# Page numbers read earlier, page sums and a cache copy moved, and the first pair's rows picked with the one-hot stationary

## The chip, the cores and the metric

The kernel runs on one core of a Trainium2 chip. The metric is the device time in microseconds (us) of one execution. The program is one hand-scheduled instruction stream per engine: TensorE (PE), VectorE (DVE), ScalarE (ACT), GpSimd (POOL) and SyncE (SP). SP issues nearly all DMAs and computes nothing. Engines wait for each other by semaphores only. All tensors are float32.

## The reference, cut to what matters

One inference step of a two-layer decoder over 264 tokens (T = 264): a prompt of 256 and 8 sample tokens. Layer 0 mixes with a state-space block, layer 1 with sparse attention (NSA), which reads a paged cache. Each layer ends in the same tail: a layer norm, a mixture of 16 experts with two experts per token, a second layer norm, and a gated per-layer embedding.

```python
def layer_tail(x, mix, p_i, ...):
    h = layer_norm(DEEPNORM_ALPHA * x + mix, ln1_g, ln1_b)
    h = layer_norm(DEEPNORM_ALPHA * h + moe(h, ...), ln2_g, ln2_b)
    return h + jax.nn.sigmoid(h @ ple_gate) * (p_i @ ple_proj)

# moe: for each expert e of 16, D = 1024, FF = 512
hid = jax.nn.silu(h @ w_gate[e]) * (h @ w_up[e])
out = out + gate[..., e:e + 1] * (hid @ w_down[e])

# layer 1, sample tokens: 8 pages of 128 rows per sequence, blocks of 64 rows
past_cmp = kv_pool[page_table, :, 0:2]
kvc = jnp.einsum('bnlckd,clk->bnckd', blocks, w)      # weighted sum over each block
```

The window cache of layer 1 comes back with its oldest row dropped and the new one added. The 511 old rows per sequence are an output copied straight from the input.

## The kernel before, in words

`tail(L)` (from L947) is run for L = 0, then the NSA stage (from L1544), then `tail(1)`. Each of these is one block: all engines meet at its end before the next begins.

A tail goes like this. The first layer norm and the router run first (L1058 to L1110). PE turns the normed activations into token rows (`turn_x`, L1072, which the trace shows as L1080), ACT copies them to SBUF (`xtok`) and stores them to the DRAM tensor `x_rows` (L1283). DVE works out, for every expert, which of 64 slots each token takes, and writes that as a one-hot matrix `sel1` (`onehot`, L1421), columns by expert and slot.

The experts are then done in 8 pairs. A pair's 128 slots need their tokens' activations as `xg` (features on the partitions, slots along the free axis). For the first pair PE gets them at once from `xtok` and `sel1` (L1115 to L1120, traced as L1119): for each of 8 feature chunks, three matmuls over the three token tiles, `xtok` as the stationary operand and 128 one-hot columns moving, which gives features by slots. ACT copies each half (4 chunks, one PSUM bank `gb[a]`) into `xg` (`pack`, L1292). For later pairs, PE computes the slots' token numbers (`slot_token`, L1108), DVE turns them into integers (`slot_gates`, L1428), POOL gathers the rows from `x_rows` with an indirect DMA (L1347), and PE turns them (`turn_rows`, L1141). The token numbers of pairs 0 and 1 are computed by six small matmuls between the first pick and the first gate product (L1121 to L1126). Those of later pairs are computed inside `up(i)`, one after each of its last steps.

Each pair is `gate(i)` (L1158, 8 steps of k, each two experts side by side in half the array's columns), `up(i)` (L1177), `turn(i)` (L1186) and `down(i)` (L1199); the result is scattered to the tokens by `scatter(i)` (L1209), added up by DVE (L1460). PE's order is in the loop at L1218. The weights come in 2 MB units through a ring of eight places. SP issues unit n + 8 when unit n's place is free, in program order (L1014 to L1028): units 8 and 9 wait for `gu_half`, which `gate(0)` signals after k = 3.

After the pairs come the second layer norm and the per-layer gate: PE makes eight tiles (L1255, m = 0 to 7), DVE takes each tile (L1523, L1524), ACT applies the sigmoid (L1336), DVE finishes the tile of `xT` (`finish`, L1514, L1516). PE may start tile m = 6 once DVE has taken tile 1.

In `tail(0)` three things for the NSA stage are mixed in. SP, after the last `down`, reads 16 page numbers from SBUF into registers (`page_number`, L1042) and loads the 8 pages of sequence 0 (`load_cmp`, L132) and two chunks of the NSA weights (L99), then, after e_done 4, the pages of sequence 1. DVE multiplies the pages of sequence 0 by the block weights (`cmp_multiply`, L136, four of them) between centring and the reciprocal of the second norm (L1502 to L1508), and sums them (`cmp_sum`, L140) one after each of the tiles m = 2 to 5. The semaphore `c_used` counts sequences summed; later page loads in the NSA stage wait for it, the ones of sequences 3 and 4 for `c_used` 1 and 2.

The NSA stage begins with DVE's loop over sequences 1 to 6 (`compress`, from L2010), POOL's multiplications for it (L136) and PE's 21 projection tiles (L1709). In `tail(1)` SP issues the copy of the old window rows, DRAM to DRAM (`win_old`, 8176 KB, L1030) after the last weights; the program's last block waits for it.

Of the kernel before, what the change touches and what calls it, by code (L numbers as in the profile page):

```python
# [20 lines left out]
P = 128  # L21
D = 1024
# [36 lines left out]
def trunk(nc, I, O):  # L59
    root = ExitStack()  # L60
    with root:
        def sem(name):
            return root.enter_context(nc.semaphore(name))
# [84 lines left out]
        router_sems = [sem("r_" + n) for n in ("log", "sig", "turn", "gate", "rank", "slots", "xtr", "xtok", "idx", "tok", "rows", "got", "over", "evac", "row0", "row1")]  # L148
# [798 lines left out]
        def tail(L, out=None):  # L947

            ld_p, e_done, e_sig, e_out, e_proj, e_pre, e_evac = ple_sems
            r_log, r_sig, r_turn, r_gate, r_rank, r_slots, r_xtr, r_xtok, r_idx, r_tok, r_rows, r_got, r_over, r_evac, r_row0, r_row1 = router_sems  # L950
# [4 lines left out]
            with ExitStack() as st:  # L955
# [26 lines left out]
                ohid = over[:, 3 * T:(3 + NF) * T].rearrange("p (f t) -> p f t", f=NF)  # L982
                rs, sgm = sgt[:, 0:2, :], sgt[:, 2:4, :]
# [28 lines left out]
                with nc.Block() as block:  # L1012
                    @block.sync
                    def _(sp):  # L1014
                        load_unit(sp, L, 3 * L, unit(3 * L))
                        sp.wait_ge(gu_half, L + 1)
# [12 lines left out]
                        if L == 1:  # L1029
                            sp.dma_start(O["win_old"], I["cache_win"][:, 1:, :]).then_inc(win_out, 16)  # L1030
# [10 lines left out]
                        if L == 0:  # L1041
                            page = [page_number(sp, n) for n in range(2 * NPG)]  # L1042
# [12 lines left out]
                    def _(pe):  # L1055
# [59 lines left out]
                        for a in range(2):  # L1115
                            for k in range(4):
                                d = 4 * a + k
                                for q, (t0, n) in enumerate(tile3):
                                    last = mm(gb[a][:, k * P:(k + 1) * P], xtok[q][0:n, d * P:(d + 1) * P], sel1[0:n, q, 0:P], start=q == 0, stop=q == 2)  # L1119
                            last.then_inc(gathered, 1)  # L1120
                        pe.wait_ge(r_gate, 2 * L + 2)  # L1121
                        pe.wait_ge(r_slots, 6 * L + 4)
                        for i in range(2):
                            for q in range(3):
                                last = slot_token(i, q, ob[0], i * (1 + NE))
                        last.then_inc(r_idx, 1)  # L1126
# [20 lines left out]
                        def gate(i):  # L1147
# [6 lines left out]
                            for k in range(KD):  # L1154
# [5 lines left out]
                                if i == 0 and k == 3:  # L1160
                                    last.then_inc(gu_half, 1)
                            last.then_inc(gu_done, 1)
# [130 lines left out]

# [1025 lines left out]
```

## Time and profile before

| | |
|---|---|
| three runs | 1116.6, 1119.33, 1121.22 us; median 1119.33 |
| profiled execution | 1118.43 us, span 1116.7 us |
| mean granted TensorE clock | 0.966 of full |
| busy share of the span | PE 93%, TensorE weight loads 57%, DVE 44%, ACT 27%, POOL 15% |
| DMA moved | 346.33 MB, mean 310 GB/s |

A busy share is a mean over stages of quite different kinds. PE's 93% says that for most of the span the time is PE's; the slices in which PE is not busy, or has half the clock, or does work of low value, are where other engines matter. The timeline lists instructions of each engine by start and duration, merged where they follow each other, and says in brackets how long the engine had been idle and who ended that.

### The profile page before, as it was taken

How to read it: one execution, taken by the hardware profiler on the slowest of the kernel's cores; microseconds unless marked ns; L12 is line 12 of the kernel's file. 1: busy time of each engine (PE TensorE's matmuls, PEld its weight loads, DVE VectorE, ACT ScalarE, POOL GpSimd, SP SyncE). 2: the span in 40 equal slices, each digit the busy share in tenths (PEclk: the TensorE clock that was granted, in tenths of full speed). 3: DMA queues.
4: the chain of work that ended last, by engine and by line, in shares of the span. 5: the costliest groups of instructions: out<-in, count | busy, mean ns of one | idle time of the engine just before them, and what ended most of it. 6: DMA issues, size and time to landing. Idle time of an engine off the chain costs nothing. (4 is left out here: it accounts for less than half of the span.)

```text
span 1116.7 us, 15016 instructions
## 1 busy us (share of the span) xinstructions
PE 1036.7 (93%) x5267; PEld 639.4 (57%) x5267; DVE 494.3 (44%) x1473; ACT 306.3 (27%) x785; POOL 167.8 (15%) x163
## 2 busy tenths in 40 slices
PE   7999998699999999999896999788999999999987
PEld 5788776488763444444475885344775443444456
DVE  1759798582531111111276996672162111111136
ACT  3111688910321111111132104462051111111124
POOL 0000002420000000000142833553000000000023
PEclk9899999899989999999998998999999999999999
DMA  9645598569429999999774975976984999999974
GB/s 317 220 160 188 154 282 276 197 226 395 189 77 396 427 429 425 428 427 427 297 301 164 394 247 166 326 244 219 428 345 151 403 429 425 428 427 426 429 313 204
DMA packets 89537, 346.33 MB, mean 310 GB/s; under 512 B 14770, under 2 KB 52658, under 8 KB 72402
## 3 DMA queue, kind: packets, MB, share of 16 engines
q1 hardware_dynamic: 82202, 321.94, 74.3%
q10 hardware_dynamic: 5240, 16.03, 3.9%
q0 software_dynamic: 2016, 7.34, 1.7%
q8 instruction: 45, 0.74, 0.3%
q14 instruction: 34, 0.28, 0.1%
HBM read 330.61 MB, written 23.04 MB: 317 GB/s over the span
## 5 line engine op out<-in xcount | busy, mean ns | idle before, releaser
L1460 DVE TENSOR_TENSOR acc<-acc,mo 128x264 f32<-128x264 f32 x64 | 27.5, 429 | 239.0 <-PE mo L1209 238.3
L518 PE MATMUL ss<-xT,expert_ring 128*128 128x264 f32 x384 | 92.9, 404 | 7.1 <-DMA expert_ring<-in_ssd_w_in 7.1
L1199 PE MATMUL mo<-expert_ring,gates_and_hidden 128*64 128x512 f32 x384 | 85.0, 595 | 8.2 <-ACT gates_and_hidden L1306 8.2
L1177 PE MATMUL mh<-expert_ring,x_packed 128*64 128x512 f32 x384 | 91.6, 603 | 0.0
L1158 PE MATMUL mh<-expert_ring,x_packed 128*64 128x512 f32 x384 | 89.1, 618 | 0.4 <-DMA expert_ring<-in_moe_w_gate 0.2
L518 PEld LDWEIGHTS ss<-xT,expert_ring 128*128 128x128 f32 x384 | 75.8, 200 | 21.4 <-issue 7.8
L1709 PE MATMUL na<-xT,expert_ring 128*128 128x264 f32 (+1 forms) x336 | 77.3, 394 | 11.2 <-PEq L1012 11.2
L1347 POOL DMA_INDIRECT x_rows_packed<-x_rows,slot_token_int x14 | 13.5, 961 | 476.6 <-DVE slot_token_int L1428 256.7
L1709 PEld LDWEIGHTS na<-xT,expert_ring 128*128 128x128 f32 (+1 forms) x336 | 64.1, 191 | 24.3 <-issue 11.9
L1469 DVE TENSOR_TENSOR gates_and_hidden<-mh,silu_gate 128x512 f32<-128x512 f32 x16 | 11.1, 691 | 132.8 <-PE mh L1177 132.8
L530 PE MATMUL ss<-xT,expert_ring 128*128 128x264 f32 x256 | 62.9, 400 | 6.3 <-ACT expert_ring_b L409 6.3
L1158 PEld LDWEIGHTS mh<-expert_ring,x_packed 128*64 128x64 f32 x384 | 29.1, 142 | 57.3 <-issue 57.2
L1199 PEld LDWEIGHTS mo<-expert_ring,gates_and_hidden 128*64 128x64 f32 x384 | 26.5, 137 | 59.1 <-issue 48.0
L530 PEld LDWEIGHTS ss<-xT,expert_ring 128*128 128x128 f32 x256 | 48.4, 194 | 19.5 <-ACT expert_ring_b L409 9.8
L1306 ACT ACTIVATE gates_and_hidden<-mo 128x512 f32<-128x512 f32 x16 | 9.6, 597 | 179.9 <-PE mo L1186 179.9
L634 PE MATMUL ss<-conv_out,expert_ring 128*128 128x264 f32 x224 | 51.4, 386 | 0.7 <-issue 0.7
L634 PEld LDWEIGHTS ss<-conv_out,expert_ring 128*128 128x128 f32 x224 | 42.5, 190 | 8.1 <-issue 0.9
L1315 ACT ACTIVATE y_slots<-mo 128x512 f32<-128x512 f32 x32 | 17.4, 594 | 101.3 <-PE mo L1199 101.3
L1209 PE MATMUL mo<-gates_and_hidden,y_slots 128*128 128x264 f32 x128 | 41.5, 406 | 3.9 <-issue 3.9
L1177 PEld LDWEIGHTS mh<-expert_ring,x_packed 128*64 128x64 f32 x384 | 24.0, 136 | 36.3 <-issue 35.5
L1255 PE MATMUL mo<-slot_onehot,expert_ring 128*128 128x266 f32 x192 | 44.4, 387 | 0.0
L136 POOL TENSOR_TENSOR expert_ring<-expert_ring,pos_softmax 128x1024 f32<-128x1024 f32 x14 | 39.0, 2811 | 23.8 <-DMA expert_ring<-in_cmp_pages 23.8
(419 smaller groups left out, 1844.2 us busy)
## 6 DMA issues: line engine op xcount, KB each, us to landing
expert_ring<-in_moe_w_down SPq DMA_DIRECT2D x24, 2048.0 KB, 18.0
expert_ring<-in_moe_w_gate SPq DMA_DIRECT2D x24, 2048.0 KB, 19.0
expert_ring<-in_moe_w_up SPq DMA_DIRECT2D x20, 2048.0 KB, 21.0
expert_ring<-in_ssd_w_in SPq DMA_DIRECT2D x9, 2048.0 KB, 7.9
expert_ring<-in_cmp_pages SPq DMA_DIRECT2D x40, 256.0 KB, 5.5
expert_ring_b<-in_moe_w_gate SPq DMA_DIRECT2D x4, 2048.0 KB, 17.4
expert_ring_c<-in_moe_w_gate SPq DMA_DIRECT2D x4, 2048.0 KB, 21.9
expert_ring<-in_moe_w_up SPq DMA_DIRECT2D x8, 1024.0 KB, 7.3
```

The source lines that it names most:

```text
L136: return eng.tensor_tensor(x, x, wb[:, a:a + 1, :].unsqueeze(1).to_broadcast([P, NPG, 2, BLK]), ALU.mult)
L518: last = mm(pt[m % 4][:, 0:T], wc[:, k, ((m - 1) % 4) * P:((m - 1) % 4 + 1) * P], xT[:, k, :], start=k == 0, stop=k == KD - 1)
L530: last = mm(z_bank[:, 0:T], wc[:, k, (j % 4) * P:(j % 4 + 1) * P], xT[:, k, :], start=k == 0, stop=k == KD - 1)
L634: last = mm(o_bank[m][:, 0:T], w_row(k)[:, m * P:(m + 1) * P], cv[:, k, :], start=k == 0, stop=k == JX - 1)
L1158: last = mm(hb[0][s * CAP:(s + 1) * CAP, :], xg[:, k, s * CAP:(s + 1) * CAP], unit(6 * i + s)[:, k * FF:(k + 1) * FF], start=k == 0, stop= ...
L1177: last = mm(hb[1][s * CAP:(s + 1) * CAP, :], xg[:, k, s * CAP:(s + 1) * CAP], unit(6 * i + 2 + s)[:, k * FF:(k + 1) * FF], start=k == 0, s ...
L1199: last = mm(ob[2 + a][s * CAP:(s + 1) * CAP, :], ht[:, k, s * CAP:(s + 1) * CAP], unit(6 * i + 4 + s)[:, o:o + 512], start=k == 0, stop=k ...
L1209: mm(sc_bank[d % 4][:, 0:T], ys[:, d * P:(d + 1) * P], sgt[:, i, :], start=True, stop=True).then_inc(sc_done, 1)
L1255: last = mm(gate_bank[m % 6][:, 0:T + 2], wc[:, k, (m % 4) * P:(m % 4 + 1) * P], scaled[:, k, :], start=k == 0, stop=k == KD - 1)
L1315: A_(ys[:, a * 512:(a + 1) * 512], ob[2 + a][:], ACT.Copy).then_inc(ys_ok, 1)
L1460: V.tensor_tensor(acc[:, d, :], acc[:, d, :], sc_bank[d % 4][:, 0:T], ALU.add).then_inc(acc_ok, 1)
L1709: last = mm(pb[m % 8][0:M, 0:T], wc[:, k, (m % 4) * P:(m % 4) * P + M], xT[:, k, :], start=k == 0, stop=k == KD - 1)
```

## The change

Five edits.

1. The first pair's rows are picked the other way round: the one-hot (128 columns) is stationary and 512 features of the token rows move, three matmuls for each half. The result is slots by features. ACT copies each half to SBUF (`x0`, a free part of `mixed`), PE turns it with four transposes into the same PSUM bank, and the old `pack` follows.
2. The six `slot_token` matmuls of pairs 0 and 1 move from before `gate(0)` into it, one after each of k = 0 to 5.
3. The copy of the old window rows is issued by SP at the start of `tail(0)`, right behind the first weight unit, not near the end of `tail(1)`.
4. SP reads the 16 page numbers right after the last weight loads of `tail(0)`, before it waits for the last `down`.
5. The four page sums of sequence 0 move from the tiles m = 2 to 5 of `tail(0)` to the start of the NSA stage, ahead of DVE's `memset`s.

```diff
                         load_unit(sp, L, 3 * L, unit(3 * L))
+                        if L == 0:
+                            sp.dma_start(O["win_old"], I["cache_win"][:, 1:, :]).then_inc(win_out, 16)
                         sp.wait_ge(gu_half, L + 1)
...
                             load_unit(sp, L, n, unit(n))
-                        if L == 1:
-                            sp.dma_start(O["win_old"], I["cache_win"][:, 1:, :]).then_inc(win_out, 16)
+                        if L == 0:
+                            page = [page_number(sp, n) for n in range(2 * NPG)]
...
                         if L == 0:
-                            page = [page_number(sp, n) for n in range(2 * NPG)]
                             load_cmp(sp, 0, page)
...
                         for a in range(2):
+                            for q, (t0, n) in enumerate(tile3):
+                                last = mm(gb[a][:], sel1[0:n, q, 0:P], xtok[q][0:n, a * 512:(a + 1) * 512], start=q == 0, stop=q == 2)
+                            last.then_inc(r_picked, 1)
+                        for a in range(2):
+                            pe.wait_ge(r_first, 2 * L + a + 1)
                             for k in range(4):
-                                d = 4 * a + k
-                                for q, (t0, n) in enumerate(tile3):
-                                    last = mm(gb[a][:, k * P:(k + 1) * P], xtok[q][0:n, d * P:(d + 1) * P], sel1[0:n, q, 0:P], start=q == 0, stop=q == 2)
+                                last = tr(gb[a][:, k * P:(k + 1) * P], x0[:, (4 * a + k) * P:(4 * a + k + 1) * P], ident[:])
                             last.then_inc(gathered, 1)
-                        pe.wait_ge(r_gate, 2 * L + 2)
-                        pe.wait_ge(r_slots, 6 * L + 4)
-                        for i in range(2):
-                            for q in range(3):
-                                last = slot_token(i, q, ob[0], i * (1 + NE))
-                        last.then_inc(r_idx, 1)
...
                                 if i == 0 and k == 3:
                                     last.then_inc(gu_half, 1)
+                                if i == 0 and k < 6:
+                                    if k == 0:
+                                        pe.wait_ge(r_gate, 2 * L + 2)
+                                        pe.wait_ge(r_slots, 6 * L + 4)
+                                    slots = slot_token(k // 3, k % 3, ob[0], k // 3 * (1 + NE))
+                                    if k == 5:
+                                        slots.then_inc(r_idx, 1)
...
+                        for a in range(2):
+                            act.wait_ge(r_picked, 2 * L + a + 1)
+                            A_(x0[:, a * 512:(a + 1) * 512], gb[a][:], ACT.Copy).then_inc(r_first, 1)
                         pack(0)
...
-                            if L == 0 and 2 <= m < 6:
-                                i1 = cmp_sum(V, 0, m - 2)
-                                if m == 5:
-                                    i1.then_inc(c_used, 1)
...
+                    for a in range(4):
+                        i1 = cmp_sum(V, 0, a)
+                    i1.then_inc(c_used, 1)
                     V.memset(kcx[:], 0.0)
```

## Rows read from the trace of the kernel before

**Rows 1.** Timeline of layer 0's first pick (start us, us, engine, line, operation, tiles).
```profile
315.08 0.61 PE L1119 MATMUL mg<-slot_onehot,x_rows_packed 128*128 128x128 f32 x4
...
319.30 0.60 ACT L1292 ACTIVATE x_packed<-mg 128x512 f32<-128x512 f32 x1 [3.63 <-PE mg L1119]
...
323.41 2.34 PE L1108 MATMUL mo<-token_and_gates,slot_onehot 128*128 128x17 f32 x12
...
335.35 4.46 PE L1177 MATMUL mh<-expert_ring,x_packed 128*64 128x512 f32 x20
```

**Rows 2.** Timeline of layer 1, the same stretch.
```profile
839.30 0.61 PE L1119 MATMUL mg<-slot_onehot,x_rows_packed 128*128 128x128 f32 x4
...
857.99 4.46 PE L1177 MATMUL mh<-expert_ring,x_packed 128*64 128x512 f32 x20
```

**Rows 3.** Chain that ended last (start us, us, what): one whole `up`, full clock.
```profile
1028.46 7.02 PE mh L1177 x32
```

**Rows 4.** Timeline: two slot_token matmuls inside up(0), and the router's transposes.
```profile
306.93 1.04 PE L1080 MATMUL mg<-ident,xT 128*128 128x128 f32 x8
...
339.74 0.40 PE L1108 MATMUL mo<-token_and_gates,slot_onehot 128*128 128x17 f32 x2
...
341.07 0.40 PE L1108 MATMUL mo<-token_and_gates,slot_onehot 128*128 128x17 f32 x2
```

**Rows 5.** Windows: length, busy us of PE, PEld, DVE, ACT, POOL, clock, DMA share, GB/s.
```profile
305.00:310.00 5.00, 5.00 (x37) 4.38 (x36) 4.52 (x22) 4.60 (x12) 0.00 (x0) 1.00 0.03 12
...
324.00:325.00 1.00, 1.00 (x7) 0.97 (x6) 0.00 (x0) 0.98 (x2) 0.00 (x0) 0.71 0.00 0
...
850.00:855.00 5.00, 5.00 (x20) 1.40 (x16) 4.42 (x5) 0.00 (x0) 0.94 (x1) 0.66 0.36 105
```

**Rows 6.** Timeline of layer 0's end, SP and ACT.
```profile
522.16 0.80 SPq L112 DMA_DIRECT2D expert_ring<-in_ple_gate  x2
...
549.44 1.08 ACT L1315 ACTIVATE y_slots<-mo 128x512 f32<-128x512 f32 x2 [7.19 <-PE mo L1199]
...
559.82 3.97 SPq L132 DMA_DIRECT2D expert_ring<-in_cmp_pages  x8
```

**Rows 7.** Timeline of layer 0's second norm and gate tiles.
```profile
567.36 0.48 ACT L1330 ACTIVATE gates_and_hidden<-mh,eps 128x264 f32<-128x264 f32 x1 [1.29 <-PE mh L1262]
...
569.05 4.63 DVE L136 TENSOR_TENSOR expert_ring<-expert_ring,pos_softmax 128x1024 f32<-128x1024 f32 x4 [4.74 <-DMA expert_ring<-in_cmp_pages]
...
573.72 1.80 DVE L1508 RECIPROCAL slot_onehot<-gates_and_hidden 128x264 f32<-128x264 f32 x1
...
577.94 7.35 PE L1255 MATMUL mo<-slot_onehot,expert_ring 128*128 128x266 f32 x32
...
582.29 1.21 DVE L140 TENSOR_REDUCE cmp_dec<-expert_ring 128x16 f32<-128x1024 f32 x1
...
595.68 0.43 DVE L1516 TENSOR_TENSOR xT<-gates_and_hidden,acc 128x264 f32<-128x264 f32 x1
...
596.44 3.86 PE L1709 MATMUL na<-xT,expert_ring 128*128 128x264 f32 x8 [11.15 <-PEq L1012]
```

**Rows 8.** Chain that ended last: layer 1's last two gate tiles, last piece.
```profile
1103.68 7.20 PE mo L1255 x32
...
1113.06 0.43 DVE xT L1516
```

**Rows 9.** Timeline of the NSA stage: DVE's multiplications for sequence 2.
```profile
613.79 4.52 DVE L136 TENSOR_TENSOR expert_ring<-expert_ring,pos_softmax 128x1024 f32<-128x1024 f32 x2 [7.33 <-DMA expert_ring<-in_cmp_pages]
```

**Rows 10.** Windows, as in Rows 5.
```profile
310.00:320.00 10.00, 10.00 (x62) 8.29 (x61) 2.59 (x15) 3.72 (x9) 0.00 (x0) 1.00 0.27 102
...
1080.00:1090.00 10.00, 10.00 (x46) 8.45 (x45) 6.23 (x11) 4.13 (x11) 6.12 (x9) 1.00 0.49 210
```

**Rows 11.** Timeline, SP: layer 0's first weight unit.
```profile
290.77 0.34 SPq L112 DMA_DIRECT2D expert_ring<-in_moe_w_gate  x1
```

**Rows 12.** The gathers, L1347: POOL's issue to landing.
```profile
DMA to landing us min/median/max: 4.6/11.6/12.5
```

More of the change, by code:

```diff
@@ L147, in trunk @@
         ln_total, ln_squares, ln_inv = [sem("ln_" + n) for n in ("total", "squares", "inv")]
-        router_sems = [sem("r_" + n) for n in ("log", "sig", "turn", "gate", "rank", "slots", "xtr", "xtok", "idx", "tok", "rows", "got", "over", "evac", "row0", "row1")]
+        router_sems = [sem("r_" + n) for n in ("log", "sig", "turn", "gate", "rank", "slots", "xtr", "xtok", "idx", "tok", "rows", "got", "over", "evac", "picked", "first", "row0", "row1")]
         moe_sems = [sem("m_" + n) for n in ("gather", "packed", "gate_half", "gate_up", "silu", "hid", "turned", "ht", "down", "ys", "scatter", "acc")]
@@ L949, in tail @@
             ld_p, e_done, e_sig, e_out, e_proj, e_pre, e_evac = ple_sems
-            r_log, r_sig, r_turn, r_gate, r_rank, r_slots, r_xtr, r_xtok, r_idx, r_tok, r_rows, r_got, r_over, r_evac, r_row0, r_row1 = router_sems
+            r_log, r_sig, r_turn, r_gate, r_rank, r_slots, r_xtr, r_xtok, r_idx, r_tok, r_rows, r_got, r_over, r_evac, r_picked, r_first, r_row0, r_row1 = router_sems
             gathered, packed, gu_half, gu_done, silu_ok, hid_ok, turned, ht_ok, down_done, ys_ok, sc_done, acc_ok = moe_sems
@@ L982, in tail @@
                 ohid = over[:, 3 * T:(3 + NF) * T].rearrange("p (f t) -> p f t", f=NF)
+                x0 = mixed[:, NP2 * T:NP2 * T + D]
                 rs, sgm = sgt[:, 0:2, :], sgt[:, 2:4, :]
```

## The prediction

> **What bounds the kernel now.** I read the chain of waits first, then the waits by engine, then the timelines of the stretches that the diff touches. The chain is PE from pair to pair: one `up` is 7.02 us of matmuls [rows 3], the other parts of a pair follow without a gap, and no weight load makes PE wait for more than a fraction of a microsecond. So in the pairs only what PE itself does counts. Three stretches are different. From the first pick to the first `up`, PE takes 335.35 - 315.08 = 20.3 us in layer 0 and 857.99 - 839.30 = 18.7 us in layer 1 [rows 1, 2], part of it at a lower clock: in the windows at 324 and at 850 the mean falls to 0.71 and 0.66, that is to the 1.2 GHz level for part of each, right when PE does the small `slot_token` matmuls and begins the gate [rows 5]. And at layer 0's end PE is done with its last gate tile at 577.94 + 7.35 = 585.3, yet starts the next stage at 596.44; DVE works until 595.68 + 0.43 = 596.1 [rows 7]. There DVE is the bound, for 11 us. Layer 1's same tail has no such tail: PE ends at 1103.68 + 7.20 = 1110.9, DVE at 1113.5, 2.6 us later [rows 8].
>
> **Edits 1 and 2, the first pick and the slot numbers.** Before, 24 matmuls of 128 columns, 48 instructions, 323.41 - 315.08 = 8.3 us, each at the price of loading 128 columns of weights; then 12 instructions of `slot_token`, 2.34 us [rows 1]; then the gate, which is 335.35 - 325.75 = 9.6 us where 16 matmuls at full clock take 7.0 [rows 3]. After: 6 matmuls, 12 instructions of 512 columns over the full width. In an `up` 32 instructions run two by two in 7.02 us, so one costs 0.43 us alone [rows 3], and 12 cost 5.2 us. ACT's copy of the first half (0.60 us [rows 1]) lies beside the second half's matmuls. The second copy does not: a handover of 0.1, 0.6, the last four transposes (half of 1.04 us for eight [rows 4]) beside the first `pack`, which itself is 0.6. The gate starts about 1.5 us after the last pick, at 6.7 us from the start.
> The six slot matmuls inside the gate: in `up(0)` two steps with one each lie 341.07 - 339.74 = 1.33 us apart [rows 4], a bare step is 7.02 / 8 = 0.88, so one costs 0.45 to 0.5 and six 2.8 us. That is more than the 1.8 to 2.3 us of doing them in one run, but nothing waits at half clock meanwhile. Gate 7.0 + 2.8 = 9.8. Sum 6.7 + 9.8 = 16.5 us. Against 20.3 and 18.7 this saves 3.8 us in layer 0 and 2.2 us in layer 1, if the clock stays at the 2.4 GHz level. If PE falls to 1.2 GHz within this stretch, as it does now, the loss comes back that the gate shows now: 9.6 - 7.0 = 2.6 us in layer 0, and some 1.6 in layer 1 (18.7 less 8.3 for the picks, 1.8 for the slot matmuls and 7.0). Then 1.2 us are saved in layer 0 and 0.6 in layer 1. I take the full clock, since the densest kind of matmul replaces the sparsest and the run of `slot_token` is gone. Bounds for both layers together: 0 (the clock low for longer than now) and 6.5 us.
> What speaks against it is the stretch with the new transposes. In the window from 305 to 310, PE did little but the router's transposes, three groups of eight, and was granted the full clock throughout [rows 4, 5]. The Trainium skill (TensorE: Matmul & The Clock Gate, Part 4: PE-mode transpose) says that transposes do not count as PE-busy the way matmuls do. By that rule, the eight transposes and the waits around them would be an idle 1.5 us, and the gate could start cold; by the row they are harmless. The row decides for me, and the rule is the first rival below.
> The slot numbers come later: `r_idx` moves from the end of the run (325.75) to gate step 5, 6.7 + 6 x 1.33 = 14.7 us after the start, 329.8, so 4 us later in layer 0 and about 4.5 in layer 1. DVE's `slot_gates`, the wide `onehot` and POOL's first gather queue behind it. The gather lands 4.6 us after issue with an idle DMA, 11.6 with weights in flight [rows 12]; it is needed after `up(0)`, at 331.6 + 8.4 + 0.5 = 340.5. Issued at 330.3 it lands between 334.9 and 341.9. I take 0.5 us of waiting over both layers, with bounds 0 and 3.
> `gu_half` comes at 6.7 + 4 x 1.33 = 12 us from the start, 5 us earlier than now; the weights start that much earlier too. No gain by itself, as PE does not wait for them.
>
> **Edit 4, page numbers.** SP is free from 523 (its last weight issue is at 522.16) and PE's last `down` ends at 549.4, but the first page load is issued at 559.82 [rows 6]: 10.4 us, nearly all of it 16 register reads. DVE waits 4.74 us for the pages, multiplies for 4.63 us and only then takes the reciprocal at 573.72, though the square root it needs was done at 567.36 + 0.48 [rows 7]. After: the reads fill SP's free time, the load is issued near 550.5 and lands, 9.2 us later as now, near 560. DVE multiplies from 564.3, where its centring ends (573.72 - 4.63 - 4.74 = 564.35), meets POOL's additions for part of it (two multiplications took 4.52 us beside POOL [rows 9], against 4.63 for four), and is done near 569.5. The reciprocal comes 4.2 us earlier.
>
> **Edit 5, the page sums.** Four reductions of 1.21 us, 1.13 from start to start of the next instruction, go from DVE between tiles 2 and 5: 4.5 us [rows 7]. With the 4.2 us above, DVE would be 8.7 us ahead, and PE is the bound: its tiles do not move, since tile 6 needs only tile 1 taken. PE ends at 585.3, DVE 2.6 us later as in layer 1 [rows 8], and the next stage's first matmul comes 0.3 us after that: 588.2 for 596.44. Saved: 8.2 us. Neither edit alone would reach that.
> What they cost in the NSA stage: DVE starts with 4.6 us of sums. It now waits 7.33 us for sequence 2's pages [rows 9], which SP loads from the stage's start and which do not depend on the sums, so the 4.6 us are hidden. `c_used` 1 is waited for by ACT, which first reads eight page numbers (some 4.5 us by the price above), and `c_used` 2 by SP behind its own reads and loads; each is late by 1 us at most. Taken as 0; if the cover were gone, 4.6 us.
> A smaller gain: PE now starts the stage after 11.15 us of idleness at half clock, 8 matmul instructions in 3.86 us [rows 7], and loses some 2 us. With 2.9 us of idleness instead it starts at full clock or comes back sooner. I take 1 us, with bounds 0 and 2.2.
>
> **Edit 3, the old rows.** In layer 1 they move at 210 GB/s with nothing beside them [rows 10]; 8.37 MB take 38 to 40 us and end around 1112, beside the first stores of y. In layer 0 they would be issued at 291, right behind the first unit [rows 11], and run until about 334. The DMA engines are nearly idle there (102 GB/s from 310 to 320 [rows 10], which is the store of `x_rows`). The cover ends at `gu_half`, 327: units 8 and 9 queue behind the last 7 us of the copy. They are needed by `up(1)` near 360, so nothing waits. At the end of layer 1, the last y store meets less traffic: 0.3 us, with bounds 0 and 1.
>
> **Sum.** 3.8 + 2.2 - 0.5 + 8.2 + 1.0 + 0.3 = 15.0 us. The profiled execution took 1118.43 us (span 1116.7 and 1.7 around it): 1103.4. It lies 0.9 us below the median of the runs, so from the median 1104.3. I say 1104. The bounds of the terms together: gain 5 to 19.
>
> **Rivals.**
> A. The clock falls in the first gate anyway, in both layers, or at the NSA stage's start. For it: it falls there now, and a wait and transposes are put just before the gate; the rule above. Against it: the row with three groups of transposes at full clock. Price 2.6 us in layer 0, 1.6 in layer 1 and part of the 1 us at the NSA stage: 1108.5.
> B. The tail's gain is given back in the NSA stage: the next stage's start is DVE's and the pages' (the loads for sequences 3 and 4 wait for `c_used`), and PE's earlier start only makes it wait before the first scores. For it: DVE there works from 613.79 on nearly without rest until PE's last projection tile. Against: its start is set by a load that the sums do not touch. Price 4.6 us: 1109.
> C. The copy of the old rows hurts, and the kernel gets slower. The place is layer 0 from 310 to 360: `x_rows` stores, the first gather and units 8 to 11 share the DMA engines with it. The Trainium skill (DMA: Bandwidth & Descriptors, Queues, rings and completion order) says that a semaphore increment lands only after every earlier write of that DMA engine, across its queues; no row here shows it. Worked out from rows: if the `x_rows` stores counted as done only with the copy, at 334, the gather would land at 346 and PE wait 5 us, 1109. It becomes a loss only if the copy holds back units 8 and 9 until more than 15 us after 360, that is if it ran until 370, at half of the 210 GB/s. Then 1119.3 + 1 or more: 1121.
> D. Edits 4 and 5 do not do what they say, because the page load waits for something else (the weight queue at 550). The windows show the queue empty from 550; the load then lands late, and only edit 5's 4.5 us are saved: 1108.
>
> **How the numbers follow.** Forecast 0.56; A 0.18; B 0.09; C mild 0.05, C as a loss 0.03; D 0.04; other misses of the kind that I can't place 0.05, half of them no change. The forecast's own range is 1100 to 1107, A, B and D reach to 1112. With the spread of the runs before (4.6 us) I give 1098.5 to 1111. Below 0.5% (5.6 us, what a measurement of this kernel can tell) no change is seen: faster means under 1113.7. Faster 0.92, same 0.04, slower 0.04.
>
> **What would show it.** In the new trace: 12 pick instructions in 5.2 us, and first pick to first `up` 16.5 us in both layers, with the granted clock at 1.00; no wait of PE for the gathered rows of pair 1; first page load near 1 us after the last `down`; reciprocal right behind the multiplications; PE's first NSA matmul 3 us after its last gate tile, for 11; DVE still waiting for sequence 2's pages. Wrong would be: a clock at 1.2 GHz in the gate (A), PE idle before the first scores (B), PE waiting on weights or rows around 340 to 365 in layer 0 (C), a late page load (D).

## The result and the profile after

The changed kernel took 1126.63 us (median of 8 runs, 1123.45 to 1132.10), the kernel before 1118.33 us beside it (8 runs, 1116.60 to 1121.22): a ratio of 1.0070, with the interval 1.0049 to 1.0091. It is 0.7% slower. The prediction was 1104 us with a range up to 1111, and 0.92 for faster; it was wrong, in sign too. The profiled execution took 1124.01 us, its span 1122.2 us, for 1116.7 before.

The page of the changed kernel: busy time of the engines, then the granted clock and the bandwidth in 40 slices (28 us each).

```profile
span 1122.2 us, 14908 instructions
...
PE 1032.4 (92%) x5211; PEld 629.2 (56%) x5211; DVE 499.2 (44%) x1473; ACT 308.1 (27%) x789; POOL 169.8 (15%) x163
...
PEclk9899999899996999999999998999999999999999
```

The reader should see one 6 in the clock's row, at the thirteenth slice (337 to 365 us). The waits of PE by line say why (us in total, times, longest):

```profile
PE mg L1140 <- DMA x_rows_packed<-x_rows,slot_token_int: 14.0, 1, 14.0
PE mo L1205 <- ACT gates_and_hidden L1315: 11.0, 16, 0.7
```

The second row is old and made of 16 short waits. The first is new, one wait of 14.0 us, for pair 1's gathered rows in layer 0. PE's timeline of layer 0 (start us, us, engine, line, operation, tiles, and in brackets the idle time before it) answers to [rows 1, 4] up to the gate's slot matmuls, and then shows that wait:

```profile
315.30 1.88 PE L1119 MATMUL mg<-x_rows_packed,slot_onehot 128*128 128x512 f32 x4
317.11 1.12 PE L1119 MATMUL mg<-y_slots,slot_onehot 8*128 8x512 f32 x2
318.16 1.98 PE L1119 MATMUL mg<-x_rows_packed,slot_onehot 128*128 128x512 f32 x4
320.08 1.12 PE L1119 MATMUL mg<-y_slots,slot_onehot 8*128 8x512 f32 x2
321.13 1.42 PE L1124 MATMUL mg<-ident,gates_and_hidden 128*128 128x128 f32 x8
322.56 1.08 PE L1157 MATMUL mh<-expert_ring,x_packed 128*64 128x512 f32 x4
323.57 0.40 PE L1110 MATMUL mo<-token_and_gates,slot_onehot 128*128 128x17 f32 x2
...
332.33 4.46 PE L1183 MATMUL mh<-expert_ring,x_packed 128*64 128x512 f32 x20
...
340.72 0.49 PE L1131 MATMUL mo<-ident,gover 128*16 128x128 f32 x3
355.21 1.97 PE L1140 MATMUL mg<-ident,x_rows_packed 128*128 128x128 f32 x8 [14.00 <-DMA x_rows_packed<-x_rows,slot_token_int]
356.97 1.06 PE L1192 MATMUL mo<-ident,gates_and_hidden 128*128 128x128 f32 x4
358.72 8.80 PE L1205 MATMUL mo<-expert_ring,gates_and_hidden 128*64 128x512 f32 x32 [0.69 <-ACT gates_and_hidden L1315]
```

Windows of the same place, with the columns of [rows 5]. The copy of the old window rows is under way from 291 to 340:

```profile
315.00:320.00 5.00, 5.00 (x13) 1.78 (x11) 0.00 (x0) 0.99 (x3) 0.00 (x0) 1.00 0.52 222
320.00:325.00 5.00, 4.88 (x22) 1.95 (x21) 0.00 (x0) 3.06 (x4) 0.00 (x0) 1.00 0.46 196
...
345.00:350.00 5.00, 0.00 (x0) 0.00 (x0) 0.00 (x0) 0.00 (x0) 1.54 (x2) 0.51 1.00 417
350.00:355.00 5.00, 0.00 (x0) 0.00 (x0) 0.00 (x0) 0.00 (x0) 0.00 (x0) 0.50 1.00 406
355.00:360.00 5.00, 4.11 (x16) 2.95 (x18) 0.00 (x0) 1.57 (x3) 0.00 (x0) 0.50 0.53 225
```

The DMA share is about 0.5 while only the copy runs: half of the 16 engines. Then PE does nothing, falls to the 1.2 GHz level (0.50) and works on at it: the `down` from 358.72 takes 8.80 us, where one at full clock takes 7.09.

Where the whole difference lies is seen when both timelines are cut at the same operations of PE. The columns no_move and wide_copy are two of the experiments below. All are us of one profiled execution; each column adds up to its span.

| stretch of PE | before | after | no_move | wide_copy |
|---|---|---|---|---|
| start to first pick, layer 0 | 315.08 | 315.30 | 315.95 | 315.61 |
| first pick to `up(0)` | 20.27 | 17.03 | 17.03 | 17.03 |
| to the turning of pair 1's rows | 8.81 | **22.88** | 8.81 | 8.82 |
| to the first gate tile of the tail | 210.10 | 213.00 | 211.41 | 211.30 |
| gate tiles to NSA's first matmul | 42.18 | 35.70 | 37.38 | 37.39 |
| NSA stage | 218.59 | 221.82 | 219.22 | 223.69 |
| layer 1 to its first pick | 24.27 | 24.26 | 24.27 | 24.27 |
| first pick to `up(0)` | 18.69 | 17.03 | 17.03 | 17.03 |
| to the first gate tile of the tail | 222.16 | 219.13 | 219.55 | 220.13 |
| to the end | 36.51 | 36.09 | 39.03 | 36.11 |

The stretches that edits 1, 2 and 4, 5 touch (first pick to `up(0)`, gate tiles to NSA) have become shorter; one stretch of 9 us has grown by 14.

### The profile page after: what moved, and what is told of

It reads as the page before. It is cut to its first block and busy times, and to the rows that moved or that the text cites. A ratio compares the mean times of both kernels' runs of the same rounds, so it can differ in the third digit from the quotient of the medians.

```text
span 1122.2 us, 14908 instructions
## 1 busy us (share of the span) xinstructions
PE 1032.4 (92%) x5211; PEld 629.2 (56%) x5211; DVE 499.2 (44%) x1473; ACT 308.1 (27%) x789; POOL 169.8 (15%) x163
## 5 line engine op out<-in xcount | busy, mean ns | idle before, releaser
L1157 PEld LDWEIGHTS mh<-expert_ring,x_packed 128*64 128x64 f32 x384 | 26.8, 137 | 47.8 <-issue 47.4
L1183 PEld LDWEIGHTS mh<-expert_ring,x_packed 128*64 128x64 f32 x384 | 24.0, 136 | 36.3 <-issue 35.4
```

Of the source, the lines that this page charges most:

```text
L1157: last = mm(hb[0][s * CAP:(s + 1) * CAP, :], xg[:, k, s * CAP:(s + 1) * CAP], unit(6 * i + s)[:, k * FF:(k + 1) * FF], start=k == 0, stop= ...
L1183: last = mm(hb[1][s * CAP:(s + 1) * CAP, :], xg[:, k, s * CAP:(s + 1) * CAP], unit(6 * i + 2 + s)[:, k * FF:(k + 1) * FF], start=k == 0, s ...
```

## The cause: what holds the gathered rows

My theory was edit 3. The gather reads `x_rows` from DRAM, so POOL may issue it only when the stores of `x_rows` have landed. POOL's timeline of the changed kernel:

```profile
344.49 1.11 POOL L1356 DMA_INDIRECT x_rows_packed<-x_rows,slot_token_int  x1 [108.83 <-DMA x_rows<-y_slots]
```

and that of the kernel before:

```profile
326.24 1.12 POOL L1347 DMA_INDIRECT x_rows_packed<-x_rows,slot_token_int  x1 [90.79 <-DVE slot_token_int L1428]
```

Before, the last thing that POOL waits for is the slot numbers, after it is a store. ACT issues the stores at the same time as ever, and SP has issued the copy 18 us earlier:

```profile
291.37 0.82 SPq L1018 DMA_DIRECT2D out_win_old<-in_cache_win  x1
```

```profile
309.25 0.33 ACTq L1289 DMA_DIRECT2D x_rows<-x_rows_packed  x1
...
312.21 0.29 ACTq L1289 DMA_DIRECT2D x_rows<-y_slots  x1
```

The trace's single packets, summed for each queue over 5 us (q1 is SP's queue, q10 ACT's, the stores; q8 carries instructions), show what happens in between:

```
310: q1: x16 1.05MB mean 2441ns max 2559; q10: x151 0.55MB mean 143ns max 162
315: q1: x16 1.05MB mean 2417ns max 2460; q10: x16 0.07MB mean 159ns max 159
320: q1: x14 0.92MB mean 2422ns max 2488; q10: x16 0.07MB mean 159ns max 159
325: q1: x18 0.83MB mean 1925ns max 2495; q8: x1 0.02MB mean 1778ns max 1778; q10: x14 0.06MB mean 159ns max 159
330: q1: x141 2.01MB mean 564ns max 2998; q10: x12 0.05MB mean 147ns max 166
```

The copy moves packets of 64 KB, 2.42 us each, 8 at a time. On the 8 engines without the copy, the stores are done in 2 us (their increments come at 311.7 to 313.3). On each of the other 8, one store packet of 4 KB (0.16 us) passes for one packet of the copy: 16 against 16 from 315 to 320, 16 against 14 behind that. `x_rows` is 264 rows of 4 KB, some 16 packets for each engine, and in the 20 us from 315 to 335 a loaded engine gets only 7 of them through (58 in the list, over 8). The rest goes when the copy thins out (its last 64 KB packet ends at 339.6), and the last increment comes at 343.7. The Trainium skill (DMA: Bandwidth & Descriptors, Queues, rings and completion order) says that each DMA engine takes turns between its queues packet by packet; these counts agree. The same page (Why a DMA increments its semaphore by 16 and not by 1) says that a DMA is spread over the largest number of engines, at most 16, that divides its slowest dimension, here 8 sequences; the trace agrees with its half share and its 8 loaded engines. I had not read the 210 GB/s of [rows 10] in that way.

Three rivals were still open: the wait comes from the other edits, by chance in one execution (a); the copy is at fault, but through the completion rule of the prediction's rival C, that is, the stores' completion counts only once the copy has ended (b); the copy's bandwidth as such is at fault (c).

### no_move: the changed kernel without edit 3

```diff
-                        if L == 0:
-                            sp.dma_start(O["win_old"], I["cache_win"][:, 1:, :]).then_inc(win_out, 16)
...
+                        if L == 1:
+                            sp.dma_start(O["win_old"], I["cache_win"][:, 1:, :]).then_inc(win_out, 16)
```

> The changed kernel with edit 3 undone (the copy of the old rows back in layer 1). Theory S (sharing: on the 8 DMA engines that carry the copy, each 4 KB packet of the x_rows stores waits for a 64 KB packet of the copy, 2.42 us, so the first gather can't start before 344): with the copy away, the 14.0 us wait of PE for the gathered rows and the 2.9 us of half clock behind it go, about 1107 to 1109. Theory T (the copy is innocent, the later slot numbers of edit 2 make the gather late): the wait stays near 14 us, about 1125. My prediction's sum for the other four edits was 14.7 us below the kernel before, 1104.

Measured: 1113.41 us (1110.08 to 1119.75, 12 runs), ratio to before 0.9966 (0.9947 to 0.9985). In its trace POOL issues the gather at 331.76, and PE does not wait for the rows. Without edit 3, 13 us come back, and (a) falls. The time expected was 1107 to 1109: the wait went, as the theory says, but the other edits gave less than was counted for them (below).

### move_only: the kernel before with edit 3 alone

The same two edits the other way round, on the kernel before.

> The kernel before with edit 3 alone. S: the x_rows stores are complete at about 344 for 314, the gather is issued at 344.5 for 326.2 and lands near 355, PE waits about 11 us before turn_rows(1) and then runs at half clock for a while (5 to 9 us lost): 1134 to 1139. T: the gather is issued at 326 as before and nothing changes: 1118.

Measured: 1132.28 us (1129.97 to 1135.56, 5 runs), ratio 1.0137 (1.0118 to 1.0157). That is 14 us for the edit alone, a little under the 1134 expected. The wait is there without any of the other edits; PE's waits by line:

```profile
PE mg L1141 <- DMA x_rows_packed<-x_rows,slot_token_int: 13.7, 1, 13.7
```

### wide_copy: the changed kernel, the copy on 16 engines, at the same early place

```diff
-                            sp.dma_start(O["win_old"], I["cache_win"][:, 1:, :]).then_inc(win_out, 16)
+                            for b in range(DB):
+                                dst, src = (x.rearrange("r c -> (r c)").rearrange("(a n) -> a n", a=16) for x in (O["win_old"][b], I["cache_win"][b, 1:, :]))
+                                sp.dma_start(dst, src).then_inc(win_out, 16)
```

> The changed kernel, the copy at the same early place but as 8 DMAs of 16 rows of 65408 B, so on all 16 DMA engines. S: at 27 GB/s for each engine the copy takes 20 us and is over near 317; the x_rows stores are complete by 320, before the gather is issued at 331; no wait, 1107 to 1109. If the copy is bound by something that 16 engines share (DRAM writes), it takes 38 us as now, now delays all 16 engines' stores, and the time stays at 1126.

Measured: 1110.94 us (1108.57 to 1113.14, 6 runs), ratio 0.9935 (0.9919 to 0.9950), 2 us above the range expected and still the lowest median of all versions. Windows from 290 on:

```profile
290.00:300.00 10.00, 8.65 (x38) 6.80 (x37) 5.47 (x21) 2.83 (x8) 0.00 (x0) 1.00 0.80 314
300.00:310.00 10.00, 9.86 (x57) 6.25 (x57) 9.24 (x31) 8.55 (x19) 0.00 (x0) 1.00 1.19 408
310.00:320.00 10.00, 10.00 (x47) 6.47 (x44) 3.05 (x18) 4.26 (x9) 0.00 (x0) 1.00 1.02 339
320.00:330.00 10.00, 9.88 (x44) 3.82 (x44) 0.00 (x0) 3.07 (x4) 0.00 (x0) 1.00 0.36 114
```

The copy's packets run from 297.7 to 323.9, 26 us where the changed kernel's take 42 (297.5 to 339.6), the stores are done at 326.1, and POOL issues the gather at 331.43, behind the slot numbers. The same bytes at the same place, moved 1.6 times as fast, make PE wait for nothing, so (c) falls as well: it is not the bandwidth. The stores are held here too. Most of them (170 of 264 rows) go only once the copy is over, 12 us later than before; it does no harm because that is still 5 us before the slot numbers.

### small_eight: the same early copy, still on 8 engines, in pieces of 4088 bytes

```diff
-                            sp.dma_start(O["win_old"], I["cache_win"][:, 1:, :]).then_inc(win_out, 16)
+                            dst, src = (x.rearrange("b r c -> b (r c)").rearrange("b (a n) -> b a n", a=128) for x in (O["win_old"], I["cache_win"][:, 1:, :]))
+                            for h in range(2):
+                                sp.dma_start(dst[:, :, 1022 * h:1022 * h + 1022], src[:, :, 1022 * h:1022 * h + 1022]).then_inc(win_out, 16)
```

> The changed kernel, the copy at the same early place and on the same 8 engines, in descriptors of 4088 B. S: the stores share each engine packet by packet with packets of their own size, and are complete by about 318 though the copy runs until about 335; no wait of PE for rows beyond 2 us, 1107 to 1110. Rival O (a store's completion is held back until the earlier writes of the same engine, across its queues, are done): the stores complete only when the copy ends, 335 or later, PE waits as now, 1122 or more.

Measured: 1150.75 us (1146.51 to 1152.71, 5 runs), ratio 1.0299 (1.0280 to 1.0318). Neither expectation had this time. The stores are no longer too late: they are done at 324.0, and POOL issues the gather at 331.22, behind the slot numbers, while the copy runs on until 372; PE waits 1.1 us for the rows. So a store's completion does not wait for the end of the copy, and (b) falls in the form in which I had used the rule. The changed kernel's own trace says the same: on its loaded engines the first store's increments come at 334.6 to 336.9, the copy's at 338.8 to 340.1. What counts is how long one packet of the neighbour is. But this kernel pays elsewhere. PE's waits by line, then SP's issues:

```profile
PE mh L1185 <- DMA expert_ring<-in_moe_w_up: 19.7, 1, 19.7
...
PE mh L1159 <- DMA expert_ring<-in_moe_w_gate: 7.8, 4, 2.7
```

```profile
327.79 25.99 SPq L112 DMA_DIRECT2D expert_ring<-in_moe_w_up  x4
353.82 5.04 SPq L112 DMA_DIRECT2D expert_ring<-in_moe_w_down  x2
```

Small pieces make the copy slow (130 to 150 GB/s in the windows at 300 and 320, stores included), the weight units queue behind it in SP's queue, and four issues of SP take 26.0 us, in the changed kernel 5.66. That is the prediction's rival C in its form as a loss, "if the copy holds back units 8 and 9". In the changed kernel itself the units were in time.

## Experiments on the other edits

### picks_only: the kernel before with edits 1 and 2

> The kernel before with edits 1 and 2 alone. From the changed kernel's trace these give 3.2 us in layer 0 and 1.7 us in layer 1 from first pick to first up: 1118.3 - 5 = 1113.3. Rival: the gain is lost again in the pairs (later gather, weights asked for earlier while the DMA queue is full): 1118.

```diff
+                            for q, (t0, n) in enumerate(tile3):
+                                last = mm(gb[a][:], sel1[0:n, q, 0:P], xtok[q][0:n, a * 512:(a + 1) * 512], start=q == 0, stop=q == 2)
...
+                                if i == 0 and k < 6:
...
+                                    slots = slot_token(k // 3, k % 3, ob[0], k // 3 * (1 + NE))
```

Measured: 1118.17 us (1116.90 to 1121.31, 12 runs), ratio 0.9998 (0.9987 to 1.0010). Nothing is gained, the rival's number, though the trace shows the two stretches shortened as in the changed kernel (`up(0)` at 332.29 for 335.35, and 17.03 us from pick to `up` in layer 1). Part of the gain goes to the late copy. Its first packets come right behind the last weights, and from its issue to its last packet pass some 67 us in each of these kernels:

| | copy issued | its last packet | last gate tile ends | last store of y issued | end |
|---|---|---|---|---|---|
| before | 1045.6 | 1112.2 | 1110.9 | 1113.5 | 1116.7 |
| picks_only | 1044.0 | 1111.5 | 1107.9 | 1110.6 | 1115.1 |
| no_move | 1038.8 | 1106.0 | 1101.7 | 1104.3 | 1109.7 |

PE's last tile comes 2.9 us earlier in picks_only, the end only 1.5 us, so the copy takes 1.4 us. The rest is lost earlier: the NSA stage takes 2.3 us more than before in this trace, and in layer 0 the pairs behind `up(0)` 1.5 us more. The last thing for which SP waits at the end is the copy; that wait of SP in no_move, then in picks_only:

```profile
SPq L2220 <- DMA out_win_old<-in_cache_win: 1.5, 1, 1.5
```

```profile
SPq L2220 <- DMA out_win_old<-in_cache_win: 0.7, 1, 0.7
```

### wide_only and picks_wide: the same question without the late copy

wide_only is the kernel before with the wide early copy of wide_copy; picks_wide adds edits 1 and 2 to it.

> The kernel before with only the copy moved to layer 0, as 8 DMAs over all 16 DMA engines. Theory S: no wait in layer 0 and a last store 0.5 to 1 us shorter: 1117.5. If moving it costs anything by itself (half-speed weights, stores), more than 1119.

Measured: 1119.20 us (1112.45 to 1121.82, 12 runs), ratio 1.0008 (0.9992 to 1.0025). Expected was 1117.5; that moving the copy gains or costs anything as long as PE and DVE end where they did can't be seen.

> wide_only with edits 1 and 2. Theory F (floor: with the late copy on 8 engines the last copy packet comes at 1111.5, behind PE's own end, so what layer 1 gains is not seen; picks_only gained nothing although its profile shows 3.1 + 1.7 us less up to the first up): without the floor the picks show 3 to 5 us: 1113 to 1115. Rival (what the picks gain is lost in the NSA stage, whichever way the copy goes): 1117 or more.

Measured: 1116.08 us (1112.88 to 1119.92, 12 runs), ratio 0.9985 (0.9968 to 1.0001). Its median is 3.1 us below that of wide_only, where the two stretches are 3.2 and 1.7 us shorter in the traces, and 1 us above the range expected. That fits an end that is no longer held, but the two intervals overlap, so it is likely and not shown.

### pages_only and pages_sums: the kernel before with edit 4, and with edits 4 and 5

```diff
+                        if L == 0:
+                            page = [page_number(sp, n) for n in range(2 * NPG)]
...
                         if L == 0:
-                            page = [page_number(sp, n) for n in range(2 * NPG)]
```

> The kernel before with edit 4 alone (page numbers read early). Theory P (the multiplications now run beside POOL's additions of squares, which delays PE by 3.4 us, but DVE stays the bound at the end of the tail because the sums are still in it): reciprocal 4.3 us earlier, next stage 4.2 us earlier, NSA stage unchanged: 1118.3 - 4.2 = 1114. Rival (my prediction's rival D: the pages land late anyway): 1118.

Measured: 1114.45 us (1111.77 to 1116.37, 6 runs), ratio 0.9958 (0.9944 to 0.9973).

```diff
-                            if L == 0 and 2 <= m < 6:
-                                i1 = cmp_sum(V, 0, m - 2)
...
+                    for a in range(4):
+                        i1 = cmp_sum(V, 0, a)
```

> The kernel before with edits 4 and 5. Prediction's sum: 8.2 + 1.0 = 9.2 us, 1109. Theory P: 8.2 less 3.4 (PE's additions of squares and the half clock behind them) gives 4.8 us at the tail, and the NSA stage, whose DVE chain and page loads are now 1 to 2.5 us later, gives 1 to 3 back: 1115 to 1117, no better than edit 4 alone.

Measured: 1113.12 us (1111.36 to 1115.43, 6 runs), ratio 0.9949 (0.9933 to 0.9965). Edit 4 alone is worth 4 us, so rival D (the load waits for something else) falls. Both are worth 5 us, for 9.2 predicted; the time lies between the two that were expected. Edit 5's own share, 1.3 us, can't be told from none. The next part shows where some of it went.

### hold_mult: no_move, with DVE's multiplications held until the squares are done

The next stage starts 3 us after PE's last tile as foreseen, but PE's tiles, from the first to the last, take 34.4 us in no_move and 31.0 before. Three timelines of no_move at that place, of DVE, POOL and PE:

```profile
563.16 6.26 DVE L136 TENSOR_TENSOR expert_ring<-expert_ring,pos_softmax 128x1024 f32<-128x1024 f32 x4
569.46 1.80 DVE L1517 RECIPROCAL slot_onehot<-gates_and_hidden 128x264 f32<-128x264 f32 x1
```

```profile
565.60 1.60 POOL L1372 TENSOR_TENSOR gates_and_hidden<-gates_and_hidden,xT 128x264 f32<-128x264 f32 x1
```

```profile
567.26 0.71 PE L1268 MATMUL mh<-gates_and_hidden,ones 128*128 128x264 f32 x2 [2.38 <-POOL gates_and_hidden L1372]
567.81 5.44 PE L1261 MATMUL mg<-slot_onehot,expert_ring 128*128 128x266 f32 x16
```

The multiplications now come while POOL adds up the squares. DVE's four take 6.26 us for 4.63 [rows 7], POOL's last addition 1.60 us for the 0.74 of the kernel before, and PE, which needs the sum of the squares for the norm, waits 2.38 us for it, 0.66 before; then it works at the 1.2 GHz level for part of the next 16 instructions (5.44 us for 3.76). The Trainium skill (GPSIMD Engine Reference, Specifications) says that POOL shares its SBUF interfaces with VectorE and that the two contend when DVE reads two SBUF inputs; these rows agree, and give the sizes. The test:

```diff
+                        dve.wait_ge(ln_squares, L + 1)
                         dve.wait_ge(ld_cmp[cmp_slot(0)], 16 * NPG)
```

> no_move with one more wait: DVE's multiplications for sequence 0 begin only when POOL has added the squares. Theory P: PE's wait before the squares' product goes from 2.4 to 0.7 us and the low clock behind it goes, PE's last gate tile ends 3.4 us earlier relative to its first; DVE becomes the bound by some 1.5 us; the next stage starts 1.8 us earlier: 1111.5. Rival (POOL's long additions come from something else): PE's wait stays at 2.4 us and the reciprocal is 2 us later, no gain: 1113.4 or more.

Measured: 1112.51 us (1109.87 to 1116.63, 6 runs), ratio 0.9947 (0.9927 to 0.9966). Its DVE and PE:

```profile
568.15 4.63 DVE L136 TENSOR_TENSOR expert_ring<-expert_ring,pos_softmax 128x1024 f32<-128x1024 f32 x4 [2.27 <-POOL gates_and_hidden L1372]
```

```profile
568.17 0.71 PE L1268 MATMUL mh<-gates_and_hidden,ones 128*128 128x264 f32 x2 [0.66 <-POOL gates_and_hidden L1372]
568.73 3.76 PE L1261 MATMUL mg<-slot_onehot,expert_ring 128*128 128x266 f32 x16
```

The old durations are back, and so are the 31 us for the tiles (30.7). That the two slow each other, and PE behind them, is shown. In return DVE is late by the time it waits, and the next stage starts 4.2 us after PE's last tile instead of 3.0: 34.9 us from the first tile to the next stage, for 37.4. The median is 0.9 us below that of no_move and 1 us above the time expected, which the runs can't tell from nothing.

### late_wide and wide_hold: towards a better kernel

late_wide is no_move with its late copy on 16 engines; wide_hold is wide_copy with the wait of hold_mult.

> no_move (edits 1, 2, 4, 5) with the copy late but over 16 engines. F: the copy is done 20 us after the weights and sets nothing; the end comes 5.1 us after PE's last gate tile, for 8.0 in no_move: 1113.4 - 2.9 = 1110.5, equal to wide_copy. Rival (the end is set by something else): 1113.

Measured: 1112.21 us (1108.18 to 1115.87, 8 runs), ratio 0.9953 (0.9934 to 0.9971). In its trace the end comes 5.07 us after the last gate tile, as with the early wide copy, for 8.0 in no_move: the copy no longer holds the end. The medians of no_move, late_wide and wide_copy (1113.4, 1112.2, 1110.9) stand in the order expected, but the intervals of neighbours overlap.

> wide_copy with the multiplications held until POOL has added the squares. hold_mult showed PE's end of the tail 3.7 us earlier relative to its first tile (30.7 us for 34.4), but the reciprocal later, and so the next stage 2.5 us earlier relative to it. Here I expect 1.5 to 2.5 us below wide_copy: 1109. Rival (the start of the NSA stage decides nothing, as its page loads set its end): 1111.

Measured: 1110.95 us (1108.01 to 1115.84, 12 runs), ratio 0.9950 (0.9933 to 0.9968). That is the rival's number, and wide_copy's median; that the two agree to a hundredth is chance, as single runs spread over 8 us. The hold brings nothing more that the runs show. Either version beats both kernels, by 7 us against the one before and by 16 against the changed one.

## Why the prediction was wrong, by its own steps

**Edit 3, the old rows: the failed step.** It counted bandwidth ("102 GB/s from 310 to 320, which is the store of `x_rows`"), looked for what queues behind the copy in SP's queue, found it harmless ("so nothing waits"), and put the edit at 0.3 us of gain. But those 102 GB/s are the very transfer on which the gather depends. It meets the copy not in a queue but on the DMA engines, where each of its small packets waits for a packet of 2.42 us. Measured: 14.0 us of waiting, 2 to 3 us of low clock behind it, in medians 13.2 us with the edit against without (1126.63 and 1113.41). Rival C, mild, had the right place and the right transfer (stores done at 334, gather 346, 5 us of waiting, chance 0.05). It was right in that the stores came last and wrong in how: they were done at 343.7, after the copy, and PE waited almost three times as long, also because the gather met the weights and needed 10.7 us to land. I called it mild because 15 us of gain stood against it; the other edits are worth 5 us as measured (no_move), so even a wait of 5 us would have left nothing.

**The end.** The prediction's 0.3 us had its bound at 1. In truth the late copy is a floor under the end: with PE earlier it holds the end back by 2.9 us in no_move and 3.2 in hold_mult (8.0 and 8.3 against 5.1 from last tile to end). What edit 3 has to gain is that, and it grows with what the other edits save.

**Edits 1 and 2.** Foreseen 16.5 us from first pick to `up`, measured 17.03 in both layers: the 12 picks take 5.8 us and not 5.2. The pitch is 0.45 us inside a run of 128-row tiles, and more where the rows change from 128 to 8 and back. Saved are 3.2 and 1.7 us, for 3.8 and 2.2. The granted clock stayed at the 2.4 GHz level through transposes and gate, so rival A failed at this place. (The row that spoke against A was read too strongly: of the 5 us from 305 to 310 the 24 transposes were 2.6, ordinary matmuls most of the rest.) The gather came from the slot numbers at 331.2 to 331.8 in no_move, wide_copy and small_eight; PE waited 0 in the first two, for 0.5 foreseen, and 1.1 in small_eight.

What these edits save in this stretch is the low clock and nothing else. The old order, at the full clock, is as short as the new: in the traces of move_only and pages_sums layer 0's stretch takes 16.99 us, with `slot_token` in 1.81 us and the gate in 7.09. So the prediction's smaller gain for the case of a low clock, 1.2 and 0.6 us, which is what the reordering itself should save, is not there. Over both layers, in ten stretches of the five kernels with the old order, two stay at the full clock and eight take 18.6 to 20.3 us; all 18 stretches of the nine kernels with the new order take 17.03. The 3.2 us in layer 0 are thus one draw of the old order: its mean over the five traces is 18.6, which makes 1.6 us.

Nor does the stretch tell what is saved later. From layer 0's first pick to its first gate tile the old order takes 237.6 to 240.0 us without the early copy on 8 engines, the new one 237.2 to 240.7, on the mean 238.9 and 238.5: what is gained before the pairs is lost in them. In layer 1 it is 240.4 to 242.3 against 236.2 to 237.7, some 4 us, more than the stretch alone. In layer 0's pairs the weights may be the limit: the DMA engines are busy throughout from 345 to 545, and PE waits for a gate's weights once, for 2.5 us in pages_sums, 1.7 in hold_mult and 1.0 in no_move. No run tests that. Alone these edits gained nothing that can be measured; what is lost to the copy, the pairs and the NSA stage is as large as what they save.

**Edits 4 and 5.** Edit 4's loads came as foreseen, and PE starts the next stage 2.96 us after its last tile for 11.15:

```profile
603.91 8.38 PE L1714 MATMUL na<-xT,expert_ring 128*128 128x264 f32 x29 [2.96 <-PEq L1013]
```

The term of 8.2 us rested on "its tiles do not move", and this failed: the prediction named the meeting with POOL's additions but priced it for DVE alone, not for POOL, and not for PE behind POOL (PE's tiles 31.0 us before, 32.8 in the changed kernel, 34.4 in no_move). From the first tile to the next stage 42.18 us became 35.7 in the changed kernel and 37.4 in no_move, 6.5 and 4.8 saved. The 1.0 us counted for a full clock at the next stage's start is borne out in no_move (granted clock 1.00 from 590 to 596, before 0.50 from 596 to 600), but not in the changed kernel (0.64 and 0.51 from 604 to 608): there rival A was right.

**Rival B, the NSA stage.** PE spent 221.8 us there for 218.6. The spread from kernel to kernel goes for a good part with one wait of PE, that for the selected pages: 0.5 to 1.5 us of it where the stage took 218.6 to 219.3 (before, wide_only, no_move, pages_sums), 4.8 to 6.6 us where it took 221.5 to 223.8 (changed kernel, pages_only, picks_wide). pages_only and picks_wide have it without edit 5, pages_sums has edit 5 and not the wait. So the sums are not its cause. wide_copy (1.2 us of that wait, 223.7 in all) and small_eight (4.6 and 219.7) fit neither. What delays those pages stays open.

Together, for the version without the harm of edit 3: 15.0 us were predicted, 7.3 were measured (wide_copy, 0.65% of the median before). The bounds of the prediction's terms add up to a gain of 5 to 18, not 19; either way they left no room for a loss, since edit 3 stood among them with 0 to 1.

## What to carry to other kernels

Before a large transfer is moved under cover, list what else is in flight there and who waits for it, small stores that a later gather reads above all; free bandwidth did not protect them here, since each small packet paid for one packet of the large transfer on its engine. Lay out a DRAM-to-DRAM copy so that all 16 DMA engines carry it, in long pieces: here it was then over in 26 us instead of 42 and did no harm at the same place, though only because it ended before the gather was due. A saving before a stretch that is full of weight loads must be read behind that stretch, and one that rests on the clock in more than one trace. When several savings are added up, look for what ends just behind the work that becomes faster (here a copy 1 us behind the last tile, and additions on POOL that slow down when DVE's multiplications come beside them).

## What the hardware showed that I had not expected

- A DRAM-to-DRAM copy with 8 as its first dimension runs on 8 DMA engines, in 64 KB packets of 2.42 us, 27 GB/s each; on 16 engines its packets took 3.0 us each and the copy 26 us for 42 (408 GB/s in the window from 300 to 310).
- 4 KB store packets of 0.16 us each, sharing an engine with that copy, passed one for one with its packets: the last was done 31 us after its issue instead of 2.
- The same copy on 8 engines in pieces of 4088 bytes took 74 us, 113 GB/s, and SP's four weight issues behind it took 26.0 us for 5.66.
- In its 14 us of waiting PE fell to 1.2 GHz at 345 and stayed there until 362; after the transposes and short waits of the new pick it stayed at 2.4 GHz. With the old pick, the same instructions fell to 1.2 GHz in eight of ten stretches and stayed at 2.4 in two.
- DVE's four multiplications of two SBUF operands beside POOL's additions: 6.26 us for 4.63, and POOL's last addition 1.60 for 0.74.
